# Scores of two layers on one Trainium2 core: one float32 block made of three rounded products of high and low parts

## The reference

```python
s = jnp.einsum('bhid,bhjd->bhij', rope(q), rope(k)) * (Dh ** -0.5)   # Dh = 128
s = jnp.where(mask, s, -jnp.inf)
p = softmax(s)                                                       # layer 2, differential: p1 - lam * p2
o = jnp.einsum('bhij,bhjd->bhid', p, v)
```

## Time and profile before

| | |
|---|---|
| time, median of 3 runs | 1800.07 us (1799.96 to 1800.71) |
| time of the profiled execution | 1799.72 us |
| its span, first to last instruction | 1797.8 us |
| PE busy | 1788.5 us (99%) |
| DVE busy | 1243.6 us (69%) |
| ACT busy | 1037.5 us (58%) |
| POOL busy | 154.5 us (9%) |
| mean granted TensorE clock | 0.999 |
| chain that ended last | PE 99% |

### The profile page before, as it was taken

How to read it: one execution, slowest core, us unless ns; L and a number is a source line. 1 busy time by engine, 2 the same in 40 slices (tenths; PEclk the granted TensorE clock), 3 DMA queues, 4 the chain that set the end, 5 groups by cost and what they waited for, 6 DMA issues and landing times.

```text
span 1797.8 us, 27226 instructions
## 1 busy us (share of the span) xinstructions
PE 1788.5 (99%) x10842; PEld 1622.1 (90%) x10842; DVE 1243.6 (69%) x1711; ACT 1037.5 (58%) x1638; POOL 154.5 (9%) x116
## 2 busy tenths in 40 slices
PE   9999999999999999999999999999999999999998
PEld 8999889888899999998889999898888999989987
DVE  6665656665666897687658888776565888767764
ACT  7435546774557765875554345576454444457853
POOL 0000000110011111100001211000000111100110
PEclk9999999999999999999999999999999999999999
DMA  9557555555555555445566655555555655555564
GB/s 370 200 171 225 182 182 190 181 175 195 190 189 167 171 171 175 154 165 169 194 207 202 199 188 176 193 180 172 190 193 196 201 199 181 174 192 183 168 220 140
DMA packets 95901, 340.30 MB, mean 189 GB/s; under 512 B 10800, under 2 KB 11184, under 8 KB 95648
## 3 DMA queue, kind: packets, MB, share of 16 engines
q1 hardware_dynamic: 94400, 334.44, 55.9%
q0 software_dynamic: 944, 3.61, 0.6%
q10 hardware_dynamic: 432, 0.53, 0.1%
HBM read 336.44 MB, written 2.10 MB: 188 GB/s over the span
## 4 chain that ended last, share of the span: by engine, by line
PE 99%; DMA 0%; DVE 0%; issue 0%; ACT 0%; DVEq 0%
PE ACC L838 15%; PE ACC L840 15%; PE ACC L839 15%; PE ACC L846 12%; PE ACC L843 12%; PE ACC L845 6%; PE ACC L844 6%; PE ACC L851 2%; PE ACC L852 2%; PE ACC L853 2%; PE PM L961 1%; PE PM L998 1%; PE PM L976 1%; PE PM L890 1%; PE PM L960 0%; PE PM L999 0%
## 5 line engine op out<-in xcount | busy, mean ns | idle before, releaser
L1654 DVE TENSOR_TENSOR WL<-RAW,WH 128x1024 fp32r<-128x1024 f32 (+2 forms) x631 | 793.4, 1272 | 421.8 <-ACT WH L1222 420.3
L1222 ACT ACTIVATE WH<-RAW 128x1024 fp32r<-128x1024 f32 (+2 forms) x632 | 646.9, 1038 | 382.5 <-PE ACC L840 190.2
L843 PE MATMUL ACC<-XHL,WH 128*128 128x512 f32 x1024 | 395.6, 386 | 0.0
L846 PE MATMUL ACC<-XHL,WH 128*128 128x512 f32 x1024 | 391.2, 382 | 0.0
L838 PE MATMUL ACC<-WH,XHL 128*128 128x512 f32 (+1 forms) x788 | 296.5, 376 | 0.0
L840 PE MATMUL ACC<-WH,XHL 128*128 128x512 f32 (+1 forms) x788 | 291.9, 370 | 0.0
L839 PE MATMUL ACC<-WL,XHL 128*128 128x512 f32 (+1 forms) x788 | 291.9, 370 | 0.0
L845 PE MATMUL ACC<-XHL,WL 128*128 128x256 f32 x1024 | 281.6, 275 | 0.0
L844 PE MATMUL ACC<-XHL,WL 128*128 128x256 f32 x1024 | 279.1, 273 | 0.0
L845 PEld LDWEIGHTS ACC<-XHL,WL 128*128 128x128 f32 x1024 | 193.5, 189 | 27.4
L844 PEld LDWEIGHTS ACC<-XHL,WL 128*128 128x128 f32 x1024 | 193.6, 189 | 26.5
(11 more groups left out here) (406 smaller groups left out, 2344.0 us busy)
## 6 DMA issues: line engine op xcount, KB each, us to landing
RAW<-in_w SPq DMA_DIRECT2D x607, 512.0 KB, 3.3
RAW<-in_wv SPq DMA_DIRECT2D x24, 344.0 KB, 3.2
X<-in_x SPq DMA_DIRECT2D x4, 512.0 KB, 11.9
Y<-in_xT SPq DMA_DIRECT2D x3, 512.0 KB, 10.6
out<-Y SPq DMA_DIRECT2D x6, 256.0 KB, 3.6
S<-in_bias POOLq DMA_DIRECT2D x8, 128.0 KB, 2.3
S<-in_od_gate_w POOLq DMA_DIRECT2D x1, 1024.0 KB, 7.1
S<-in_final_norm POOLq DMA_DIRECT2D x1, 1024.0 KB, 6.3
```

The lines of the kernel that those rows point to most:

```text
L843: e.matmul(acc[0], wh0, pairs, start=f, stop=False, skip_group_check=True)
L846: m = e.matmul(acc[1], wh1, pairs, start=False, stop=l, skip_group_check=True)
L1222: e.activation(hi, src, ACT.Copy).then_inc(s_hi)
L1654: e.tensor_tensor(lo, src, hi.bitcast(F32), ALU.subtract).then_inc(s_lo)
```

## The change

For heads 8 to 39 the second scores matmul (second queries by all keys) is no longer one float32 matmul. A new step "halves", three slots ahead of a head's scores, makes rounded high parts of the second queries (128x128) and of the keys (128x256) on ACT, and low parts, value minus high part, on POOL. PE then multiplies high by high, high by low and low by high into the same place of PSUM, after a wait for both low parts. The first matmul stays float32. The parts lie in two sets in HALF, which takes the first 1536 columns of what was SC.

```diff
--- before.py
+++ after.py
@@ -191,7 +191,9 @@
             RAW = [sb(f"RAW{i}", 1024, F32, first) for i in range(NRAW)]
         WL = [sb(f"WL{i}", 1024, F32R) for i in range(NRAW)]
         WH = [sb(f"WH{i}", 1024, F32R) for i in range(NHL)]
-        SC = sb("SC", 4096)
+        with ExitStack() as first:
+            SC = sb("SC", 4096, F32, first)
+        HALF, _ = sb("HALF", 1536, F32R), sb("SC_REST", 2560)
         C = sb("C", CW)
         ZC = sb("ZC", 1024)
         S5 = sb("S5", 2048)
@@ -270,6 +272,11 @@
         def qk_slot(g):
             return SC[:, 512 * (g % 3):512 * (g % 3) + 512]
 
+        def half_slot(a):
+
+            at = 768 * (a % 2)
+            return [HALF[:, at + x:at + y] for x, y in ((0, 128), (128, 256), (256, 512), (512, 768))]
+
         def sc_slot(g):
             return SC[:, 1536 + 384 * (g % 3):1920 + 384 * (g % 3)]
 
@@ -455,12 +462,15 @@
                         late = 1 if first == 24 and step[0] == "p" else 0
                         put(slot + every * r + late, step, first + h + (4 if step[0] == "p" else 0), 1)
                         if step == "scores":
+                            if first >= 8:
+                                put(slot + every * r - 3, "halves", first + h)
                             put(slot + every * r, "rsum", first + h)
                             put(slot + every * r + 0.5, "normal", first + h)
 
         def pairs_plan(slot):
 
             for a in range(8, 16):
+                put(slot + 4 * (a - 8) - 3, "halves", a)
                 put(slot + 4 * (a - 8), "scores", a, 1)
             for i in range(4):
                 g = 4 + 9 + 2 * i
@@ -645,7 +655,7 @@
             sem(n) for n in ("s_one", "s_sel", "s_dgz", "s_dgh", "s_dgl", "s_dgt", "s_mdh", "s_mdl", "s_mdt", "s_zc"))
         s_dg, s_pa, s_pe, s_pk, s_pc, s_pm, s_zero, s_am, s_tri, s_la = (
             sem(n) for n in ("s_dg", "s_pa", "s_pe", "s_pk", "s_pc", "s_pm", "s_zero", "s_am", "s_tri", "s_la"))
-        s_neg = sem("s_neg")
+        s_neg, s_hh, s_hl = sem("s_neg"), sem("s_hh"), sem("s_hl")
         s_lx, s_lc, s_ly, s_ld, s_so, s_sd, s_sa, s_or, s_on, s_gd1 = (
             sem(n) for n in ("s_lx", "s_lc", "s_ly", "s_ld", "s_so", "s_sd", "s_sa", "s_or", "s_on", "s_gd1"))
         s_lg, s_li, s_lxg, s_le, s_lq, s_ls, s_zs, s_zg, s_zh, s_zl = (
@@ -958,7 +968,14 @@
                     qT, kT = feat(3 * n)[:, h, :], feat(3 * n + 1)[:, h, :]
                 o = bank(b)
                 e.matmul(o[:, 0:128], qT[:, 0:128], kT[:, 0:128], start=True, stop=True)
-                e.matmul(o[:, 128:384], qT[:, 128:256], kT, start=True, stop=True).then_inc(s_sc)
+                if a < 8:
+                    e.matmul(o[:, 128:384], qT[:, 128:256], kT, start=True, stop=True).then_inc(s_sc)
+                else:
+                    qh, ql, kh, kl = half_slot(a)
+                    e.wait_ge(s_hl, 2 * (a - 8) + 2)
+                    e.matmul(o[:, 128:384], qh, kh, start=True, stop=False)
+                    e.matmul(o[:, 128:384], qh, kl, start=False, stop=False)
+                    e.matmul(o[:, 128:384], ql, kh, start=False, stop=True).then_inc(s_sc)
                 read_out[b] = (s_msk, masked(a))
 
             def pT(g, b):
@@ -1376,6 +1393,15 @@
                 e.activation(qk[:, 0:256], PM[b][:, 0:256], ACT.Copy, scale=qks).then_inc(s_qk)
                 e.activation(qk[:, 256:512], PM[b][:, 256:512], ACT.Copy).then_inc(s_qk)
 
+            def halves(a, _):
+                layer, n, h = head_of(a)
+                qh, _, kh, _ = half_slot(a)
+                e.wait_ge(s_rot, ROPE.index(J_OF[layer, f"k{n}", h // 2]) + 1)
+                if a > 9:
+                    e.wait_ge(s_sc, a - 1)
+                e.activation(qh, feat(3 * n)[:, h, 128:256], ACT.Copy).then_inc(s_hh)
+                e.activation(kh, feat(3 * n + 1)[:, h, :], ACT.Copy).then_inc(s_hh)
+
             def scores(a, b):
                 sc, c = sc_slot(a + 4), cols(a + 4)
                 e.wait_ge(s_mx, 2 * a + 1)
@@ -1593,7 +1619,7 @@
 
             steps = {"seed": seed, "warm": warm, "xt": xt, "squares": squares, "root": root, "rms_a": rms_a, "gates1": gates1, "selectors": selectors, "decay_cols": decay_cols,
                      "decay_rows": decay_rows, "cols": columns_step, "rows": rows, "decay": decay, "pT": pT,
-                     "norm_qk": norm_qk, "qkT": qkT, "scores": scores, "normal": normal, "silu_z": silu_z, "yT": yT, "mix1": mix1, "pv": pv, "ty": ty, "copied": copied, "silu": silu, "decays1": decays1,
+                     "norm_qk": norm_qk, "qkT": qkT, "halves": halves, "scores": scores, "normal": normal, "silu_z": silu_z, "yT": yT, "mix1": mix1, "pv": pv, "ty": ty, "copied": copied, "silu": silu, "decays1": decays1,
                      "decays2": decays2, "norm_sq": norm_sq, "norm_sum": norm_sum, "turn_v": turn_v, "delta_a": delta_a, "tri": tri, "small_x": small_x,
                      "spread_t": spread_t, "level_x": level_x, "level_y": level_y,
                      "solve4": solve4, "onorm": onorm, "gate_lru": gate_lru, "decay_lru": decay_lru, "root_lru": root_lru,
@@ -2232,6 +2258,14 @@
                     e.wait_ge(s_msk, 2 * a + 2)
                     load_bias(a + 2)
 
+            def halves(a, _):
+                layer, n, h = head_of(a)
+                qh, ql, kh, kl = half_slot(a)
+                e.wait_ge(s_hh, 2 * (a - 8) + 1)
+                e.tensor_tensor(ql, feat(3 * n)[:, h, 128:256], qh.bitcast(F32), ALU.subtract).then_inc(s_hl)
+                e.wait_ge(s_hh, 2 * (a - 8) + 2)
+                e.tensor_tensor(kl, feat(3 * n + 1)[:, h, :], kh.bitcast(F32), ALU.subtract).then_inc(s_hl)
+
             def gate_z(i, _):
                 e.wait_ge(s_zT, ZT.index(J_OF[3, "zg", i]) + 1)
                 e.wait_ge(*finished(24 + 2 * i + 1))
@@ -2285,7 +2319,7 @@
                     e.wait_ge(s_evD, at_D(3, "out", b) - 1 + t)
                     e.tensor_tensor(Y3[:, t, c], X3[:, t, c], S0[:, c], ALU.mult).then_inc(s_gn)
 
-            steps = {"norm_qk": norm_qk, "scale_k": scale_k, "scores": scores, "gate_z": gate_z, "cols": columns_step, "tri": tri, "gate_w": gate_w,
+            steps = {"norm_qk": norm_qk, "scale_k": scale_k, "halves": halves, "scores": scores, "gate_z": gate_z, "cols": columns_step, "tri": tri, "gate_w": gate_w,
                      "gate_lru": gate_lru, "gate_c": gate_c, "load_mask": load_mask, "load_gain": load_gain, "gained": gained}
 
             def go(todo):
```

## The result

The changed kernel takes 1806.89 us (median of 6 runs, 1806.38 to 1807.83) against 1800.43 us for the kernel before (6 runs): the ratio is 1.0036, 95% interval 1.0023 to 1.0048, or 6.5 us more. The forecast was 1807.0. The profiled execution took 1806.93 us, with a span of 1805.1 us at a granted clock of 0.999.

A forecast was written before the change was run, and what follows sets the result against it. PE was taken to bound the kernel, busy 1788.5 of 1797.8 us. Saving -3.3, heads 8 to 15 +4.7 and heads 24 to 31 +5.5 gave +6.9 on 1799.72; with 0.35 for the median, 1807.0, range 1802.5 to 1814.

The forecast's parts named there:

- Ring and wait in heads 24 to 31: Halves behind the exp delay ACT and DVE 0.5 us a head; PE waits for low parts and loses 5.5 us.
- the ring: Heads 24 to 31: ACT waits for DVE's row maximum, DVE for ACT's WH; 13.1 us a head before the change.
- Heads 8 to 15: POOL and DVE take turns, the second WL starts 0.5 us late, low parts come 5.5 after the exp; PE loses 4.7.
- the WH's share: Heads 8 to 15: WH, itself 0.5 us later, would alone have let the second WL start only 0.3 late.
- rival C: Heads 8 to 15: no contention of POOL and DVE, chain +0.3 us a head, low parts 3.4 after exp; 1803.7, chance 0.15.
- the 4 to 6 us a stretch: Sign of being right: PE idle ahead of the first product, 4 to 6 us in heads 8 to 15 and 24 to 31 each.
- PE's saving: Second scores matmul, heads 8 to 39: three products of 0.11 us replace 0.44 us; 3.3 us saved over 32 heads.
- ACT's price: Two copies per head, 128x128 and 128x256, cost ACT's queue 0.20 + 0.31, 0.5 us a head.
- The sum: Whole kernel: -3.3 + 4.7 + 5.5 = +6.9 us, 1806.6 on the profiled execution, 1807.0 as median.
- B's WL of 2.4 us: Heads 8 to 15, sign of rival B: POOL takes both turns before the second WL, or is slower; 1810.1, chance 0.17.
- C's waits from head 24 only: Sign of the no-contention rival: PE waits on POOL only from head 24 on, none in heads 8 to 15.
- Rival A: All stretches: low parts come in time and only PE's saving is left, 1796.8 us; chance 0.08.

The follow-up runs named there:

- no_pool: The changed kernel without POOL's two subtractions, the products waiting for and taking high parts in place of low ones: 1803.85 us against 1800.26 before, ratio 1.0021.
- idle_act: The changed kernel with halves 4.5 slots ahead of the scores instead of three, in ACT's idle time: 1798.02 us against 1800.26 before, ratio 0.9988.
- early7: The changed kernel with halves seven slots ahead of the scores instead of three: 1802.3 us against 1800.33 before, ratio 1.0011.
- unused_halves: The changed kernel making the parts but not reading them, PE keeping the one float32 matmul without a wait: 1804.27 us, ratio 1.0022 to before.

## Why the prediction held, step by step

**Ring and wait in heads 24 to 31: right.** Halves 3.17 us after the exp, 0.5 us a head on the ring, exp to exp 13.6, waits from head 28 on of at most some 1.6, a loss of 5.5: the trace has 3.17, 0.50, 13.62, the four heads, 1.5 to 1.6 at most, 5.4. The experiments show the cause: with POOL away the ring is as late (no_pool), with ACT's copies in its idle time it is not late at all (idle_act).

**Heads 8 to 15: the mechanism right, one step wrong; 3.3 instead of 4.7.** The step said that POOL and DVE take turns and that the second WL therefore starts 0.5 us late, near 1.7. The timelines at head 15, of ACT, DVE and POOL:

```profile
1110.63 0.40 ACT L1408 ACTIVATE SC<-SC,SM 128x128 f32<-128x128 f32 x1 [1.01 <-DVE SM L1888]
...
1112.67 0.40 ACT L1403 ACTIVATE HALF<-S 128x256 fp32r<-128x256 f32 x1
...
1112.60 1.22 DVE L1680 TENSOR_TENSOR WL<-RAW,WH 128x1024 fp32r<-128x1024 f32 x1 [1.02 <-ACT WH L1239]
1114.06 1.23 DVE L1680 TENSOR_TENSOR WL<-RAW,WH 128x1024 fp32r<-128x1024 f32 x1 [0.23 <-ACT WH L1239]
...
1112.84 1.30 POOL L2265 TENSOR_TENSOR HALF<-S,HALF 128x128 fp32r<-128x128 f32 x1 [6.00 <-ACT HALF L1402]
1114.11 1.76 POOL L2267 TENSOR_TENSOR HALF<-S,HALF 128x256 fp32r<-128x256 f32 x1
```

POOL does wait for each WL, 1.30 and 1.76 us instead of 0.45 and 0.72. But the second WL waits 0.23 for its WH and takes 1.23: POOL's first, held until the first WL ended at 1113.82, was over at 1114.14, and DVE stood waiting for its WH for most of that time. So the chain grows by 0.32 a head and not 0.5 (a pair of exps is 25.48 apart, before 24.84), just what the text gave as the WH's share ("would have allowed 0.3") and as rival C's chain, and no_pool shows the same chain without POOL's subtractions; the low parts are there 5.24 us after the exp (1115.87 less 1110.63), near the forecast's 5.5 and not C's 3.4. Six heads at 0.18 less are 1.1, and 0.26 for the readiness: together the 1.4 by which the term was too large; 3.3 is also below the 4 to 6 us a stretch that was to show the forecast right. The waits came at heads 13 and 15 instead of from 11 on. The Trainium skill ("Perfetto Trace Analysis", Optimizing Scalar/DVE Operations) says that GpSimd and VectorE share a read port, which a two-port VectorE operation locks for itself, so that moving work between them may not help. The longer subtractions (1.30 and 1.76 us) agree with a shared port. No run moves them to DVE, so the advice stays untested here; idle_act shows only that the overlap costs nothing where the low parts come 2.2 us and more before PE wants them.

**PE's saving: 2.5 instead of 3.3.** The products start 0.12 us apart (1569.35, 1569.47, 1569.59; over all heads 0.118, 0.119), where the step took the 0.11 of L844 to L846. Three products thus take about 0.02 more a head, most of the 0.026 that are missing (3.3 / 32 less 0.077). Why they are slower than the pieces' products of equal width is open; no run tried it.

**ACT's price: right.** The halves last 0.294 and 0.401 us and hold the queue for 0.5. The durations are those of the estimate from the Trainium skill ("VectorE: DVE Perf Modes", The TRN2 errata), 0.29 and 0.40. What the queue loses is less than the 0.69 of the two together: 0.50 us, and exp to exp grew by 0.51.

**The sum: near, and the last 0.4 us are luck.** The traces give 3.3 + 5.4 - 2.5 = 6.2 where the forecast had 4.7 + 5.5 - 3.3 = 6.9: the loss in heads 8 to 15 was put 1.4 too high and the saving 0.8, and the two misses cancel in part. The medians say 6.5. The time is right within 0.1 us (1806.89 against 1807.0) only because the kernel before, at 1800.07 in the three runs that the forecast was built on, has a median of 1800.43 in six.

**The rivals.** B's WL of 2.4 us and C's waits from head 24 only did not come. Rival A priced low parts that come in time at the saving alone, 1796.8. That price was wrong by 5.5: early7 is that case and takes 1802.3, since the late ring reaches PE through the rope read-out as well (4.4 of the 5.5; the rest is the saving, 0.8 too large, and the median of before). Only where the ring isn't delayed either, in idle_act, is nearly the saving alone left, 2.2 us. The text named the ring's delay and didn't ask what is late next once the low parts are not.

## What to carry to other kernels

What work for a partly idle engine costs depends on where it stands in the queue, and not on its length alone: the same two ACT copies, 0.5 us a head, cost 4.0 us and more behind the exp of a ring (unused_halves, early7, no_pool), and 0.3 to 0.4 us 1.5 slots earlier, in the wait ahead of the exp. Before moving a producer forward because its consumer waits, look whether the producer also delays the chain; early7 took away the wait and kept 4.4 of the 8.7 us. Price "in time" by what the next consumer of the same chain then waits for.

## What the runs showed of the hardware that was not expected

POOL's subtraction of 128x128 takes 0.45 us and of 128x256 0.72 to 0.74, with an output in the rounded format, as long as no WL of DVE runs; beside one that began first it takes up to 1.49 (idle_act) and 1.77, and doesn't lengthen it (1.22 to 1.23 at head 15 of the changed kernel). The WL that is lengthened there is one that comes while a POOL operation is running: the second one beside the 512-column rope add, 3.44 for the two instead of 2.36. A short subtraction lengthens a WL as well where it comes first: at head 8 of the changed kernel, one begun at 1022.62 keeps the WL begun at 1022.76 for 1.48, and the three WL in a row there take 4.84 where they took 4.58 before. Over the whole span DVE's busy time grew by only 0.9 us (1243.6 to 1244.5). So a short POOL operation that comes upon a long DVE operation costs the chain of DVE nothing in these runs.
